# Two raw units at the head of both modulated stages, and a new order ahead of rotary attention

## The reference, cut to what matters

```
mod = silu(c) @ w_ada + b_ada
sh1, sc1, g1, sh2, sc2, g2 = split(mod, 6)
u = rmsnorm(h, norm1_w) * (1 + sc1) + sh1
proj = u @ w_in                      # q, f, i, g of the recurrence, q, k, v of the attention
h = h + g1 * (mix @ w_out)
u = rmsnorm(h, norm2_w) * (1 + sc2) + sh2
h = h + g2 * ((silu(u @ w_gate) * (u @ w_up)) @ w_down)
```

## Time and profile before

| | |
|---|---|
| median of 3 runs | 1973.14 us (1970.89 to 1973.36) |
| the profiled execution | 1972.97 us, span of its instructions 1970.8 us |
| TensorE busy | 1904.0 us, 97% |
| VectorE, ScalarE, GpSimd busy | 55%, 47%, 7% |
| chain that ended last | TensorE 92%, VectorE 3%, ScalarE 2% |
| mean granted TensorE clock | 0.989 |

### The profile page before, as it was taken

The page is one execution under the profiler, slowest core; times in us unless marked ns, Lnnn a source line. Parts: engine busy times, 40 slices in busy tenths (PEclk is TensorE's granted clock), DMA queues, the critical chain, the costliest instruction groups (busy, mean ns, idle before and its releaser), DMA issues.

```text
span 1970.8 us, 25056 instructions
## 1 busy us (share of the span) xinstructions
PE 1904.0 (97%) x8914; PEld 1533.2 (78%) x8914; DVE 1082.2 (55%) x1640; ACT 928.4 (47%) x1520; POOL 138.5 (7%) x132
## 2 busy tenths in 40 slices
PE   7999999999999899999999999889999879999997
PEld 6777778888788677778888878668887658888886
DVE  5566554444466767755444455577776554444322
ACT  5555543323477444444434367556555344343322
POOL 0000020000021000010000013211011100000000
PEclk9999999999999999999999999999999989999999
DMA  3111123232455322223232355511122122323331
GB/s 136 65 64 64 43 93 103 93 103 89 134 195 192 105 86 90 87 76 99 86 105 85 104 170 189 183 64 58 66 70 65 65 74 86 105 85 104 89 98 62
DMA packets 56478, 193.65 MB, mean 98 GB/s; under 512 B 7136, under 2 KB 7648, under 8 KB 56416
## 3 DMA queue, kind: packets, MB, share of 16 engines
q1 hardware_dynamic: 47712, 163.60, 25.5%
q0 software_dynamic: 7696, 27.79, 4.3%
q10 hardware_dynamic: 1008, 1.45, 0.2%
HBM read 186.52 MB, written 2.10 MB: 96 GB/s over the span
## 4 chain that ended last, share of the span: by engine, by line
PE 92%; DVE 3%; ACT 2%; issue 1%; DMA 1%; SPq 0%; ACTq 0%; POOL 0%; DVEq 0%
PE ps L360 27%; PE ps L361 26%; PE ps L362 26%; PE ps L2009 1%; PE ps L1896 1%; PE ps L956 1%; PE ps L1877 1%; PE ps L981 1%; PE ps L1912 1%; PE ps L971 1%; PE ps L1900 1%; DVE xl L937 1%; PE ps L2057 0%; PE ps L2044 0%; PE ps L2083 0%
## 5 line engine op out<-in xcount | busy, mean ns | idle before, releaser
L360 PE MATMUL ps<-xh,whi 128*128 128x512 f32 x1536 | 608.5, 396 | 22.9 <-DVE xl L937 16.6
L362 PE MATMUL ps<-xh,wlo 128*128 128x512 f32 x1536 | 600.7, 391 | 0.0
L361 PE MATMUL ps<-xl,whi 128*128 128x512 f32 x1536 | 600.3, 391 | 0.0
L345 DVE TENSOR_TENSOR wlo<-raw,whi 128x1024 fp32r<-128x1024 f32 (+1 forms) x296 | 365.5, 1244 | 231.3 <-ACT whi L334 225.7
L334 ACT ACTIVATE whi<-raw 128x1024 fp32r<-128x1024 f32 (+1 forms) x304 | 312.0, 1036 | 170.0 <-PE ps L362 169.1
L360 PEld LDWEIGHTS ps<-xh,whi 128*128 128x128 f32 x1536 | 289.8, 189 | 93.1 <-issue 16.8
L362 PEld LDWEIGHTS ps<-xh,wlo 128*128 128x128 f32 x1536 | 289.9, 189 | 61.3
L361 PEld LDWEIGHTS ps<-xl,whi 128*128 128x128 f32 x1536 | 290.1, 189 | 59.6 <-issue 1.4
L360 PE MATMUL ps<-acth,whi 128*128 128x512 f32 x528 | 213.0, 403 | 0.0
L362 PE MATMUL ps<-acth,wlo 128*128 128x512 f32 x528 | 208.6, 395 | 0.0
L361 PE MATMUL ps<-actl,whi 128*128 128x512 f32 x528 | 208.3, 394 | 0.0
(11 more groups left out here) (296 smaller groups left out, 2230.8 us busy)
## 6 DMA issues: line engine op xcount, KB each, us to landing
raw<-in_gu SPq DMA_DIRECT2D x132, 512.0 KB, 3.3
raw<-in_down SPq DMA_DIRECT2D x48, 512.0 KB, 3.7
raw<-in_qkv SPq DMA_DIRECT2D x24, 512.0 KB, 4.3
wada<-in_ada POOLq DMA_DIRECT2D x24, 512.0 KB, 3.7
tmps<-in_ada POOLq DMA_DIRECT2D x24, 512.0 KB, 3.6
raw<-in_qkvb SPq DMA_DIRECT2D x24, 512.0 KB, 3.6
raw<-in_down SPq DMA_DIRECT2D x24, 384.0 KB, 3.1
raw<-in_recur SPq DMA_DIRECT2D x16, 512.0 KB, 3.3
```

The costliest lines, as they stand in the source:

```text
L345: eng.tensor_tensor(wlo[:, s, 0:n], raw[:, s, 0:n], whi[:, s, 0:n].bitcast(F32), ALU.subtract).then_inc(lo_done, 1)
L360: pe.matmul(ps[:, bank], whi[:, s, w], hi[:, k0 + k], start=start and k == 0, stop=False)
L361: pe.matmul(ps[:, bank], whi[:, s, w], lo[:, k0 + k], start=False, stop=False)
L362: mm = pe.matmul(ps[:, bank], wlo[:, s, w], hi[:, k0 + k], start=False, stop=stop and k == n - 1)
```

## The change

Three parts. In duo, the first two units (f and q) are made from raw activations: xh and xl hold h times the feature scale, without the token factor and the shift; they are made in down1, tile by tile behind the squares. The factor is applied when the unit is taken out, and the shift comes in as a bias: its product with the unit's weights is made by 32 products of two columns (`shift_products`: the shift's high and low part; two units, 8 k, whi and wlo). The modulation proper starts behind the taking out of f, and xh and xl are overwritten tile by tile behind q's products (`raw_read`). In gu2 it is the same for its units 0 and 1 (gate and up), with the raw tiles made in mix. The sums of squares are made within the first raw unit (ahead of k 5, `midway`), and the shift products ahead of k 7 (`late`). Splits of units 2 and 3 move ahead, into the stage before and into the norm; in duo their slots are 3 and 2.

Ahead of rotary attention the last `ada_product` moves behind yl 1, the variance from behind yl 3 to behind yl 1, the rest of the norm from behind yl 5 to behind yl 3; the high part of qkvb's unit 2 is made ahead of yh 5, its low part behind the taking out of unit 0, and the two `ada_tile` products behind unit 1.

```diff
-                if k == 4 and midway is not None:
+                if k == 5 and midway is not None:
                     midway()
+                if k == n - 1 and late is not None:
+                    late()
...
+        def raw_hi(act, r, m, scale):
+            act.activation(xh[:, m], h[:, m], ACT.Copy, scale=scale[:, bass.ds(m, 1)]).then_inc(r.x_hi.sem, 1)
+        def raw_lo(dve, r, m, scale):
+            wait(dve, r.x_hi, m + 1)
+            dve.scalar_tensor_tensor(xl[:, m], h[:, m], scale[:, bass.ds(m, 1)], xh[:, m].bitcast(F32),
+                                     ALU.mult, ALU.subtract).then_inc(r.x_lo.sem, 1)
...
+        def shift_products(pe, u, n, bank):
+            pe.wait_ge(shift_lo, n + 1)
+            for j in range(2):
+                pe.wait_ge(lo_done, u.number(0, j) + 1)
+                for k in range(KT):
+                    w = slice(k * P, (k + 1) * P)
+                    for part in (whi, wlo):
+                        mm = pe.matmul(ps[:, bank, 2 * j:2 * j + 2], part[:, u.slot(j), w], shifts[n][:, k, :],
+                                       start=k == 0 and part is whi, stop=k == KT - 1 and part is wlo, skip_group_check=True)
+                mm.then_inc(biased, 1)
+        def biases(dve, n, bank, sign):
+            dve.wait_ge(biased, 2 * n + 2)
+            dve.tensor_copy(bias_parts, ps[:, bank, 0:4]).then_inc(bias_step, 1)
+            dve.wait_ge(bias_step, 3 * n + 1)
+            dve.tensor_scalar(bias[:, 0:1], bias_parts[:, 0:1], bias_parts[:, 1:2], sign, ALU.add, ALU.mult)\
+               .then_inc(bias_step, 1)
+            dve.tensor_scalar(bias[:, 1:2], bias_parts[:, 2:3], bias_parts[:, 3:4], 1.0, ALU.add, ALU.mult)\
+               .then_inc(bias_step, 1)
...
+            wait(pe, r.h_new, 5)
+            product(pe, u, 0, 0, 0, xh, xl, ready=r.x_lo, midway=lambda: total(pe, r, 7),
+                    late=lambda: shift_products(pe, u, 1, 5))
+            wait(pe, r.h_new, 6)
+            product(pe, u, 0, 1, 1, xh, xl, read=raw_read)
...
         def modulate_act(act, key, shift, tmp, u, between=None):
+                if m == 3 and between is not None:
+                    between()
                 act.wait_ge(n_scaled[key], m + 1)
+                if m < KT - 1:
+                    act.wait_ge(raw_read, read_before[key] + m + 1)
+                else:
+                    act.wait_ge(mm_done, u.number(0, 1) + 1)
...
             dve.scalar_tensor_tensor(twin[:, :], ps[:, 6], 1.0 / D, var[:, :], ALU.mult, ALU.add).then_inc(twin_var.sem, 1)
+            split_lo(dve, U["duo"], (0, 3))
...
-            modulate_dve(dve, "1", scale1, 0, twin)
+            raw_out("f", 2, kd)
+            biases(dve, 0, 5, -1.0)
+            modulate_dve(dve, "1", scale1, 0, twin, (tmp[3], tmp[4]))
...
                 if more:
                     gate_first(n)
+                if n == 0:
+                    stage_norm()
...
                     difference(n, (0, 1))
+                if n == 0:
+                    raw_out("q", 3, qd)
+                    refine_rest(dve, r1f)
+                    shift_low(dve, 1)
...
-            res_dve(dve, U["mix"], r2a, None, modulation=16, regain="final1", begun=2, banks=EARLY_MIX)
+            res_dve(dve, U["mix"], r2a, None, modulation=16, regain="final1", begun=2, banks=EARLY_MIX, refined=False,
+                    raw=scale2, extra=lambda: split_lo(dve, U["gu2"], (0, 2)))
+            refine_var(dve, r2a, 7)
+            split_lo(dve, U["gu2"], (0, 3))
+            refine_rest(dve, r2a)
             wait(dve, r2a.rstd, 4)
-            modulate_dve(dve, "2", scale2, 24, rstd)
-            ffn_dve(dve, U["gu2"], f2, scaled=False)
+            biases(dve, 1, 5, 1.0)
+            modulate_dve(dve, "2", scale2, 24, rstd, (tmp[0], tmp[1]))
...
+                if j == 0:
+                    product(pe, u, 0, j, 2, xh, xl, ready=r1f.x_lo, midway=lambda: twin_totals(pe),
+                            late=lambda: shift_products(pe, u, 0, 5))
+                    for part_of in (4, 5):
+                        ada_tile(pe, 1, 3, part_of)
+                    return
+                if j == 1:
+                    product(pe, u, 0, j, 3, xh, xl, read=raw_read)
+                    return
...
-            pool.wait_ge(mm_done, u.first)
+            wait(pool, twin_total, 2)
```

More of the change, by code:

```diff
@@ L86, in __init__ @@
         self.last = False
+        self.places = tuple(range(ring))
     def per(self, slot):
@@ L164, in build @@
         work = small[:, 66:96]
+        bias_parts, bias = small[:, 34:38], small[:, 38:40]
         where = {}
@@ L363, in product @@
                                stop=stop and k == n - 1)
+                if read is not None and k < n - 1:
+                    mm.then_inc(read, 1)
             if k == n - 1:
@@ L664, in body @@
                         split_hi(act, u, ahead(u, t, j, end))
+                    if extra is not None and end and j == u.body - 1:
+                        extra()
                     if ada is not None:
@@ L813, in ffn_pe, with raw_ffn_pe, body @@
             body(0)
+            with pe.Fori(1, u.count) as t:
+                body(t)
+        def raw_ffn_pe(pe, u, f, r, key):
+            def body(t):
+                for j in range(4):
+                    wait(pe, f.up, 2 * t + (j // 2 - 1))
+                    product(pe, u, t, j, j, xh, xl, ready=n_lo[key] if leading(t) and j == 2 else None)
+            wait(pe, r.h_new, 5)
[3 more added lines that the diff above has]
+            product(pe, u, 0, 1, 1, xh, xl, read=raw_read)
+            for j in (2, 3):
+                product(pe, u, 0, j, j, xh, xl, ready=n_lo[key] if j == 2 else None)
             with pe.Fori(1, u.count) as t:
@@ L1212, in _, with rope_hi @@
                     root(act, r0f)
+                    split_hi(act, U["qkvb"], (0, 2))
             u = U["qkvb"]
+            def rope_hi(t):
+                for j in range(3):
+                    if not leading(t) or j:
+                        split_hi(act, u, ahead(u, t, j, False))
             def output_hi(s, t):
@@ L1313, in _ @@
                     head_root(2 * t - 1)
-                if more:
+                if t >= 0 and more:
                     high("f", n)
```

210 lines of the change are left out of this document (142 added, 68 removed).

## The result

The changed kernel takes 1960.97 us (median of 4 runs, 1959.78 to 1961.81), the kernel before in the same session 1973.25 (1970.89 to 1973.87): ratio 0.9936, 95% interval 0.9924 to 0.9949. That is -12.3 us where -2.5 was forecast, outside the range.

The account below looks back on a forecast made before the run. TensorE, busy 97% of the span, was taken to bound the kernel, so only waits at three stage heads could be saved. Terms -1.4 - 0.5 - 0.6 = -2.5 gave 1970.5 us, range 1965 to 1977.7.

Parts of the forecast that it names:

- recurrence head: After down1: level products at 1324.4 against 1325.83, -1.4 us; ends -3.5 and +2.2.
- gu2 head: Mix into gu2: third unit ends 1.6 earlier, less 1.1 for clock, -0.5 us; ends -5.6 and +3.1.
- rotary head: Head of rotary attention: scores come 0.6 earlier through SP's queue, -0.6 us; ends -1.5 and +0.5.
- The queue terms: Mix and gu2: unit 4 3.6 later, loop 5.3 a unit, h 7 at 1584.6, TensorE waits 3.8 for the sum.
- my bound of -1.5: Rotary attention: the lower end given for its -0.6 us term.
- Dear shift products: Rival, both 32-product groups: slower kernel, at 0.224 us each +4.7, 1977.7 us; chance 0.15.
- cheap ones: Rival, both shift product groups: at 0.06 us each, 1.7 more saved per group, -5.9, 1967.1 us; chance 0.08.
- the first rival: VectorE and ScalarE queues cost less than added up: -6.5, 1966.5 us; chance 0.28.

Follow-up runs that it names:

- the change at the old addresses: Changed kernel with its two shift tiles placed behind the last tile, so all other tiles keep the addresses of the kernel before: 1969.96 us, ratio 0.998.
- the gap alone: Kernel before with 128 unused bytes ahead of wada and nothing else: 1959.37 us, ratio 0.9925.
- both moves: Kernel before with all tiles 128 bytes higher and another 128 unused bytes ahead of wada: 1958.48 us, ratio 0.9923.
- gap 128 with the rotary part: Kernel before with 128 unused bytes ahead of wada and, of the change, only the rotary attention hunks: 1958.99 us, ratio 0.9927.

## Why the prediction was wrong, and where it was right

**The step that failed is one that is not there.** The part-by-part sum has a recurrence head, a gu2 head and a rotary head, and no term for the 128 bytes that all tiles behind `small` move. It was in the diff, and the trace of before showed the handle: 0.227 us between products with xh, 0.2325 between those with acth, oh and yh. I used one number, 0.231, for both. None of the rivals had it either: all of them argued over queues, waits and the price of shift products. The missing term measures -14.0 by itself, 1.6 of it in clock at the recurrence. The forecast of -2.5 was for the reordering, and that measures -3.4 (-5.9 to -2.2) at the addresses for which it was worked out. That this is near is in part luck: in the profiles the recurrence gave -2.1 where -1.4 was forecast, gu2 +0.5 where -0.5 was, and two misses of opposite sign cancel; 0.4 us lies outside the span of instructions (2.2 us around it before, 1.8 here), for which the sum had nothing.

**The recurrence, forecast -1.4.** From down1's last product to the level products it is 53.66 us before, 51.60 with the change at the old addresses (-2.1), 52.06 with the gap alone and 53.03 with both (+1.0). Step by step in the changed kernel: unit f follows after 0.23 (0.3 forecast). The shift products took 0.111 each at full clock, and 0.214 for the last ones, when the clock fell; 3.8 to 4.0 us in all (3.6). The first modulation step is 13.6 behind down1's last product, before 8.5: +5.1 (+4.2); the forecast had no fall of the clock ahead of it, and the last five shift products and f's k 7 at half clock are most of the 0.9. The gate is 25.65 behind it, before 25.42: +0.2 instead of -1.0, as much too late as the modulation. v is 39.7 behind, before 42.2: -2.5 (-3.5). TensorE waited 6.74 us for i's take-up by ScalarE (the reading of unit i's bank) and then had to turn it; I had put the whole wait of some 7 us on unit 4's low part, which was ready at 1303.3, just before the turn was over. GpSimd's product lay beside the last norm step (1.64 instead of the 0.69 of the step ahead of it), so 0.9 of contention (1.1 charged). The clock after the wait was 0.73, and from v to the level products it took 1.9 us longer than before (2.1 taken):

```profile
1303.67:1311.14 7.47, 7.47 (x27) 5.97 (x25) 7.40 (x18) 6.62 (x10) 0.71 (x1) 0.73 0.44 138
```

as forecast from the earlier trace rows. But a wait does not by itself bring this loss. With the gap alone the same wait of 2.48 us ahead of g was followed by full clock:

```profile
1298.94 0.47 PE L361 MATMUL ps<-xh,whi 128*128 128x512 f32 x1 [2.48 <-DVE wlo L346]
```

```profile
1298.94:1305.90 6.96, 6.96 (x33) 5.78 (x34) 6.89 (x13) 6.42 (x12) 1.01 (x1) 1.00 0.47 153
```

Over all kernels with this wait (2.4 to 2.5 us) it is not a matter of one profile: the five with a distance other than 0 have 0.76 or 0.77 in the 7.1 us behind it, the three with distance 0 (gap 128, both moves, gap 128 with the rotary part) have 1.00. Each has one profile. How the addresses, or the earlier times that they bring, do this is not shown; it is 1.6 us, and with it the kernel without the reordering came out ahead.

**gu2, forecast -0.5.** From the level products to the fourth unit of gu2: 282.60 before, 283.09 with the change at old addresses (+0.5); 281.84 with the gap, 282.86 with both (+1.0). The queue terms were right: unit 4 of mix +3.2, counted from the last unit of duo (3.6), the loop 5.23 a unit (5.3), h 7 4.5 behind mix's last product (4.5), a wait of 3.6 ahead of the sum (3.8), 3.8 for the shift products (3.6). The modulation starts 15.9 behind mix's last product (1585.62; 14.0 forecast, and 1.1 put apart for the clock), and then there is what was not counted. Its first high copy overwrites xh 0, which the second raw unit must have read:

```profile
1585.62 1.41 DVE L1037 SCALAR_TENSOR_TENSOR tmps<-h,small,rstd 128x512 f32<-128x512 f32 x2
...
1587.93 0.72 ACT L1057 ACTIVATE xh<-tmps,mod 128x512 fp32r<-128x512 f32 x1 [6.89 <-PE ps L371]
1589.21 0.72 ACT L1057 ACTIVATE xh<-tmps,mod 128x512 fp32r<-128x512 f32 x1 [0.56 <-PE ps L371]
```

VectorE's product for it began at 1585.62 and took 0.7, so the wait for the reader is 1.6 us. It is a new dependence that the edit brings, and it fell in a stretch at half clock, where the reader is slow.

**Rotary attention, forecast -0.6.** The scores came 1.6 earlier at the old addresses, just past my bound of -1.5, and 0.9 earlier at the new ones. The loop then gave much of it back; o_b starts 0.45 and 0.8 earlier, near the forecast. The timed run of this part alone cannot tell it from nothing.

**The rivals.** Dear shift products are ruled out (0.111 each, where they would have decided from 0.151), and cheap ones too (0.06). The Trainium skill (TensorE: Matmul & The Clock Gate, Back-to-back issue gap) has about 81 ns for a pair of load and product at 128 columns; the level products of 128 columns show 112 here, and the shift products of two columns 111. The time fell where the first rival put it (faster by more than 0.2%), but not by its mechanism. "Queues cost less" was wrong where I could follow it: they cost what the rows said.

## What to carry to other kernels

Read the start-to-start distance of like instructions for each tile they read, not one mean for the engine: two numbers for one operation are a lever. When a diff inserts bytes ahead of other tiles, it changes every one behind them; give that a line in the sum, and time the bare gap as the first experiment. A small tile can be kept out of the way by placing it last.

## What the runs showed of the hardware that was not expected

- Products of 128x512 with an fp32r moving operand start 0.227 us apart if it lies at the same place modulo 256 bytes as the weights, 0.229 at 64 above, 0.2325 at 128 and 0.233 at 192. It is the same where no other engine and no DMA is at work. Only multiples of 64 bytes were tried (64, 192 and the move of all tiles in one run each), with the PSUM banks unchanged; 14.0 us of this kernel hang on it, 1.6 of them through the clock.
- Stretches at 1.2 GHz come and go at the same place of the program, at 1.6 us each: after the same wait three kernels kept 1.00 and five had 0.76 or 0.77, and ahead of mix four of fourteen profiles lack a stretch that ten have. The changed kernel's mean granted clock is 0.986 where it was 0.989, by an estimate some 5.7 us of full clock more lost (1.4% of 1959.3 less 1.1% of 1970.8). A difference of 2 us between two profiles may be one such stretch: find it in the windows before giving the time to the edit.
- A VectorE operation with two SBUF inputs took 1.25 us beside a GpSimd addition and 0.74 without it, for the same instruction on the same tiles.
